# The copies of the rope outputs to the heads are issued by ACT, behind the weight splits, instead of by the sync engine

## The chip, the cores and the metric

The kernel runs on one core of a Trainium2 chip. A core has five engines with instruction streams of their own: TensorE (PE, matmuls), VectorE (DVE), ScalarE (ACT), GpSimd (POOL) and the sync engine (SP), and 16 DMA engines that move what the engines' streams tell them to. The metric is the time of one execution on the device, in microseconds; lower is better.

## The reference

Two blocks follow each other on 256 tokens of width 1024. The first has two layers, and it is in these that the change lies. Cut to what matters:

```python
def hybrid_layer(x, norm_g, w_in, ...):
    h = rmsnorm(x, norm_g)
    proj = h @ w_in        # q and k of three kinds of attention, v, gates
    ...
    # every q and k: apply_rope(heads(t, n), cos, sin)
    #   x1, x2 = halves of a head of 64; [x1*c - x2*s, x1*s + x2*c]
    ya = moba_attention(...); yb = dsa_attention(q, k, v, iq, ik, iw); yc = dilated_mixture(...)
    return x + merged @ w_out
```

dsa_attention needs index scores of iq and ik for all tokens before it can choose its 64 keys each. The second block (feed-forward, Fourier and retention layers, with conditioning rows from ada_w) is untouched.

## The kernel before

All matmuls are in fp32 precision made of two halves: a weight tile is split in a high part (w_high, by ACT) and a low part (w_low, by POOL), and TensorE does three products per pair. The weights stream through a ring of four slots (RING). A chunk of the stream goes SP load to raw (chunk, L476), ACT split to w_high (split, L603), POOL subtraction to w_low (L1107), 24 matmuls L1984 to L1986 (12 matmuls L2033 to L2035 for a v chunk). The load of chunk m waits for lo_done of chunk m - 4, the split waits for landed of its slot and for chunk_done of chunk m - 4. ACT and POOL work three chunks ahead (AHEAD).

A layer is a chain of such phases: qk (24 chunks, six laps of four), vn (12 v chunks), mix (32 chunks interleaved with the softmax units), br, out. In qk, DVE turns each pair of result banks into rope outputs (rotate, L1279 to L1284) in the tile rot, and multiplies rows of ada_w between them (modulate, L1289 and L1293). rot holds head halves by chunk; the attention needs whole heads of 64 rows on one side of the partitions. So small SBUF to SBUF copies move rot to heads: for each group g of four chunks eight copies of 32 partitions (heads_of, L496, 64 KB each), six groups per layer, and four copies of 32 KB for the last index key tile (L536). All 52 add to the semaphore heads_in. Before, SP issues them in one piece per group between the weight loads: groups 0 to 2 in the qk laps 3 to 5, groups 3 to 5 and the four last copies in the three vn laps. The loads of the first mix chunks stand behind these in SP's order.

In vn DVE also makes the normed input again: normed_scaled (L1416) for tile k, then ACT's high part (L769, two tiles behind the splits of v chunks 7 to 10), then DVE's low part (L1422). At the end of vn TensorE waits for all copies of the layer, `e.wait_ge(heads_in, 832 * L + 832)` (L2075), and computes the index scores (L2090). ACT applies relu (L773, L776), which stands in its order behind the splits of mix chunks 0, 1 and 2, and the first mix chunk on TensorE waits for the first relu (`relu_done`), since it uses the bank.

Of the kernel before, what the change touches and what calls it, by code (L numbers as in the profile page):

```python
# [30 lines left out]
RING = 4  # L31
AHEAD = 3
# [7 lines left out]
W8 = ((CW, LINE),) * RING  # L40
WIDE = ((CW, 0),) * RING
WV = ((2 * VW, 0),) * RING
# [9 lines left out]
QK, VN, GATE, MIXG, BR, OUT = 24, 12, 8, 24, 8, 8  # L52
# [104 lines left out]
@contextmanager  # L157
def turns(eng, count, *tallies):

    kept = [(t, t.base, t.n) for t, _ in tallies]  # L160
    with eng.Fori(0, count) as i:
        for t, k in tallies:
            t.base = t.base + i * k
        yield i
    for (t, base, n), (_, k) in zip(kept, tallies):
        assert t.n - n == k, (t.n - n, k)
        t.base, t.n = base, n + k * count


def program(nc, xT_d, cols_d, cond_d, ada_d, w1_d, wv_d, wu_d, wd_d, w2_d, rope_d, mask_d, ident_d, identb_d,  # L170
            dft_d, rope2_d, dist_d, out_d):
    with ExitStack() as ctx:
# [274 lines left out]
        def of_layer(name, L):  # L447
            m, d, a, n = hybrid[name]
            return m + L * PER_LAYER, d + L * PER_D, a, n
# [18 lines left out]
        def _(e):  # L468
# [18 lines left out]
                e.dma_start(ada[:, slot, :], ada_d[bass.ds(r, 1)].rearrange("a p n -> p (a n)"))\  # L487
                    .then_inc(ada_landed[slot], 16)

            def heads_of(d0, g):  # L490

                e.wait_ge(emptied_d, 4 + d0 + RING * g + RING)
                for jq in range(4):
                    for r in range(2):
                        dst = 64 * (jq % 2) + 32 * r
                        e.dma_start(head_tiles[dst:dst + 32, bass.ds(2 * g, 2), jq // 2, :],  # L496
                                    rot_tiles[32 * jq:32 * jq + 32, bass.ds(2 * g, 2), r, :]).then_inc(heads_in, 16)

            head_tiles = heads[:, 0:NPOS // 2, :].rearrange("p (g a) t -> p g a t", a=2)
            rot_tiles = rot[:, :, :].rearrange("p (g a) t -> p g a t", a=2)  # L500
            per = PER_LAYER - VN
            for L in range(LAYERS):
                m0, d0, _, _ = of_layer("qk", L)
                w0, r0 = per * L, ADA_L * L
                for j in range(RING):
                    chunk(m0 + j, j, W8, w1_d, w0 + j)
                    if L == 0 and j == 0:
                        for k in range(4):
                            e.dma_start(x[:, 0, 2 * k:2 * k + 2, :], xT[:, 2 * k:2 * k + 2, 0:T]).then_inc(x_in[k], 16)
                if L:  # L510
                    e.wait_ge(ada_done, 2 + r0)
                e.dma_start(ada[:, :, :], cond_d).then_inc(cond_in, 16)
                if L == 0:
                    for dst, src in ((rope[:, :, :], rope_d.rearrange("p (a t) -> p a t", a=2)),
                                     (ident[:, :], ident_d), (identb[:, :], identb_d), (mask[:, :], mask_d)):
                        e.dma_start(dst, src).then_inc(consts_in, 16)
                for i in range(1, QK // RING):
                    for j in range(RING):
                        chunk(m0 + RING * i + j, j, W8, w1_d, w0 + RING * i + j)
                        if j % 2:  # L520
                            if i == 1 and j == 1:
                                e.wait_ge(c_silu, 2 * L + 2)
                            ada_row(r0 + 2 * (i - 1) + j // 2, j // 2)
                    if i >= 3:
                        heads_of(d0, i - 3)
                m1 = m0 + QK
                for i in range(VN // RING):
                    for j in range(RING):
                        chunk(m1 + RING * i + j, j, WV, wv_d, VN * L + RING * i + j)
                        if i == 0 and j % 2:  # L530
                            ada_row(r0 + ADA_L - 2 + j // 2, j // 2)
                    heads_of(d0, QK // RING - 3 + i)
                for jq, half in ((2, 1), (3, 0)):
                    for r in range(2):
                        dst = 64 * half + 32 * r
                        e.dma_start(heads[dst:dst + 32, NPOS // 2, :],  # L536
                                    rot[32 * jq:32 * jq + 32, QK - 2 + r, :]).then_inc(heads_in, 16)
                load(m1 + VN, 2 * RING, W8, w1_d, w0 + QK)
                if L == LAYERS - 1:
                    e.wait_ge(ada_done, 2 + ADA_H)  # L540
                    e.dma_start(x[:, 1, :, :], xT[:, :, T:2 * T]).then_inc(context_in, 16)
                load(m1 + VN + 2 * RING, MIX + BR + OUT - 2 * RING, W8, w1_d, w0 + QK + 2 * RING)
# [51 lines left out]
        def _(e):  # L594
            n_sq, n_scaled, n_shifted = Tally(), Tally(), Tally()

            def split(lap, mm, c, width):

                e.wait_ge(landed[c % RING], 16 * lap + 16)
                if not (isinstance(mm, int) and mm < RING):  # L600
                    e.wait_ge(chunk_done, 1 + mm - RING + 1)
                w, at_ = width
                e.activation(wh[:, c % RING, at_:at_ + w], raw[:, c % RING, 0:w], ACT.Copy).then_inc(hi_done, 1)  # L603
# [24 lines left out]
            def stepped(base, widths, after, first, count, before=None, behind=None):  # L628

                m0, _, _, n = base  # L630
                for k in range(first, first + count):
                    i, j = divmod(k, RING)
                    c = j + AHEAD
                    w = after if k + AHEAD >= n else widths
                    if before:
                        before(k)
                    split(hybrid_lap(m0) + i + c // RING, m0 + RING * i + c, c, w[c % RING])
                    if behind:
                        behind(k)
# [7 lines left out]
            def to_hh(k, q):  # L647
                return flat(hh, k, T * q, T)


            def table_for_sqrt():
                e.activation(spare[:, 4:5], eps[:, :], ACT.Sqrt)
# [79 lines left out]
            for L in range(LAYERS):  # L732
                def laps(name):
                    lap_of[0] = hybrid[name][0] // RING + L * (PER_LAYER // RING)
                    return of_layer(name, L)
# [17 lines left out]
                stepped(laps("qk"), W8, WV, 0, RING, roots, silu_of_cond)  # L753
                i_end = QK // RING - 1
                m0 = laps("qk")[0]
                with turns(e, i_end - 1) as i:
                    for j in range(RING):
                        c = j + AHEAD
                        split(lap_of[0] + i + 1 + c // RING, m0 + RING + RING * i + c, c, W8[0])
                stepped(laps("qk"), W8, WV, RING * i_end, RING)  # L760


                m0 = laps("vn")[0]
                for c in range(AHEAD, VN + AHEAD):
                    split(lap_of[0] + c // RING, m0 + c, c, WV[0] if c < VN else W8[0])
                    if 0 <= c - TILES_FROM < KT // 2:
                        for k in (2 * (c - TILES_FROM), 2 * (c - TILES_FROM) + 1):
                            e.wait_ge(scaled, n_scaled())
                            e.activation(hh[:, k, 0:T], ps[:, 6 + k % 2, 0:T], ACT.Copy).then_inc(norm_hi, 1)  # L769
# [1944 lines left out]
```

## Time and profile before

| | us |
|---|---|
| median of 3 runs | 2269.53 (2267.81 to 2269.68) |
| the profiled execution | 2268.79 |
| its span in the trace | 2267.0 |
| PE busy | 2211.4 |
| DVE, ACT, POOL busy | 1124.1, 830.8, 1342.6 |

The page's header gives the span. Busy time is the union of an engine's instruction times; matmuls are pipelined, so a busy PE need not be at its peak. Register, semaphore and DMA-issuing instructions don't count as busy. Layer 0 has its qk and vn phases from 14 to 112 us, layer 1 from 305 to 402 us.

### The profile page before, as it was taken

Reading aid. Unit: us, or ns where it says so; the run is one execution under the profiler, and the core shown is the slowest. Engines: PE = TensorE matmul, PEld = TensorE weight load, DVE = VectorE, ACT = ScalarE, POOL = GpSimd, SP = SyncE. Lnnn points to the kernel's source line nnn. Section 1 sums busy time; section 2 is a strip of 40 time slices with the busy share of each in tenths; the row PEclk is TensorE's granted clock in tenths of the full one; section 3 lists DMA queues with packets and bytes.
Section 4 is the critical chain, followed back from the end, with each engine's and each line's share of the span. In section 5 each row is a group of like instructions: output and inputs, shape, how many; then the busy total and the mean of one; then the engine's idle time right before and its main releaser. Section 6 shows DMA issues by size and latency. Waiting matters only on the chain.

```text
span 2267.0 us, 39013 instructions
## 1 busy us (share of the span) xinstructions
PE 2211.4 (98%) x13460; PEld 1971.0 (87%) x13460; DVE 1124.1 (50%) x2117; ACT 830.8 (37%) x1270; POOL 1342.6 (59%) x704
## 2 busy tenths in 40 slices
PE   8989999899999999999999999999999999999999
PEld 7989999898888888878888888888888988999999
DVE  6754568544665543277655423655522511243653
ACT  5355453554532222243222222322222413665444
POOL 6765787648665554323655544555544644558997
PEclk9999999999999999999999999999999999999999
DMA  8842468523365543312655432555533422225555
GB/s 289 276 152 96 147 242 278 189 90 131 117 238 200 196 147 95 103 66 86 223 186 199 137 103 92 203 192 185 195 90 95 163 103 102 103 84 186 182 169 159
DMA packets 112399, 356.35 MB, mean 157 GB/s; under 512 B 13224, under 2 KB 21928, under 8 KB 111920
## 3 DMA queue, kind: packets, MB, share of 16 engines
q1 hardware_dynamic: 112304, 355.07, 46.5%
q8 instruction: 61, 1.00, 0.2%
q14 instruction: 34, 0.28, 0.0%
HBM read 347.40 MB, written 1.05 MB: 154 GB/s over the span
## 4 chain that ended last, share of the span: by engine, by line
PE 82%; DVE 6%; issue 4%; POOL 3%; ACT 2%; DMA 1%; SPq 1%; DVEq 0%; POOLq 0%; ACTq 0%
PE ps L1984 22%; PE ps L1985 22%; PE ps L1986 22%; POOL w_low L1107 3%; PE ps L2033 1%; PE ps L2035 1%; PE ps L2034 1%; PE ps L2152 1%; PE ps L2485 1%; PE ps L2120 1%; DMA raw<-in_w_dram 1%; DVE ps L1347 1%; PE ps L2185 1%; PE ps L1996 1%; SPq L496 1%
## 5 line engine op out<-in xcount | busy, mean ns | idle before, releaser
L1107 POOL TENSOR_TENSOR w_low<-raw,w_high 128x1024 fp32r<-128x1024 f32 (+3 forms) x542 | 1200.3, 2224 | 663.7 <-ACT w_high L603 662.6
L603 ACT ACTIVATE w_high<-raw 128x1024 fp32r<-128x1024 f32 (+3 forms) x544 | 537.3, 989 | 1060.6 <-PE ps L1986 823.3
L1984 PE MATMUL ps<-h_high,w_high 128*128 128x256 f32 (+2 forms) x2704 | 889.2, 329 | 16.9 <-DVE rot L1284 5.1
L1985 PE MATMUL ps<-h_low,w_high 128*128 128x256 f32 (+2 forms) x2704 | 879.4, 325 | 0.0
L1986 PE MATMUL ps<-h_high,w_low 128*128 128x256 f32 (+2 forms) x2704 | 879.2, 325 | 0.0
L1984 PEld LDWEIGHTS ps<-h_high,w_high 128*128 128x128 f32 x2704 | 511.8, 189 | 65.3 <-DVE rot L1284 6.1
L1985 PEld LDWEIGHTS ps<-h_low,w_high 128*128 128x128 f32 x2704 | 512.8, 190 | 42.9
L1986 PEld LDWEIGHTS ps<-h_high,w_low 128*128 128x128 f32 x2704 | 513.0, 190 | 42.6
L1984 PE MATMUL ps<-act_high,w_high 128*128 128x512 f32 (+1 forms) x770 | 266.2, 346 | 0.0
L1985 PE MATMUL ps<-act_low,w_high 128*128 128x512 f32 (+1 forms) x770 | 265.6, 345 | 0.0
L1986 PE MATMUL ps<-act_high,w_low 128*128 128x512 f32 (+1 forms) x770 | 265.6, 345 | 0.0
L1188 POOL TENSOR_TENSOR act_low<-hn,act_high 128x512 f32 (+3 forms) x88 | 101.8, 1157 | 213.2 <-DVE act_high L1636 205.6
L1633 DVE TENSOR_TENSOR hn<-tn,ps 128x512 f32<-128x512 f32 x66 | 45.4, 689 | 287.0 <-PE ps L1986 258.1
L1984 PEld LDWEIGHTS ps<-act_high,w_high 128*128 128x128 f32 x770 | 145.1, 188 | 18.3
L1985 PEld LDWEIGHTS ps<-act_low,w_high 128*128 128x128 f32 x770 | 145.1, 188 | 18.1
L1986 PEld LDWEIGHTS ps<-act_high,w_low 128*128 128x128 f32 x770 | 145.1, 188 | 18.0
L1306 DVE SCALAR_TENSOR_TENSOR sq<-ada,ps 128x1024 f32<-128x1024 f32 x120 | 146.5, 1221 | 17.2
L1302 DVE SCALAR_TENSOR_TENSOR sq<-ada,ps 128x1024 f32<-128x1024 f32 x120 | 146.1, 1218 | 9.6 <-DMA ada<-in_ada_dram 1.3
L1661 DVE SCALAR_TENSOR_TENSOR x<-ps,gate,x 128x256 f32 (+1 forms) x49 | 21.8, 481 | 257.1 <-PE ps L1986 256.7
L1996 PE MATMUL ps<-h_high,w_high 128*128 128x256 f32 (+1 forms) x264 | 79.3, 300 | 15.1 <-DVE h_low L1245 7.8
L2033 PE MATMUL ps<-w_high,h_high 128*128 128x512 f32 (+1 forms) x224 | 83.7, 373 | 2.0 <-POOL w_low L1107 2.0
L2035 PE MATMUL ps<-w_high,h_low 128*128 128x512 f32 (+1 forms) x224 | 83.3, 372 | 0.0
(243 smaller groups left out, 2272.8 us busy)
## 6 DMA issues: line engine op xcount, KB each, us to landing
raw<-in_w_dram SPq DMA_DIRECT2D x216, 512.0 KB, 3.4
raw<-in_wu_dram SPq DMA_DIRECT2D x176, 512.0 KB, 4.2
ada<-in_ada_dram SPq DMA_DIRECT2D x144, 512.0 KB, 3.6
raw<-in_wd_dram SPq DMA_DIRECT2D x64, 384.0 KB, 3.1
raw<-in_wd_dram SPq DMA_DIRECT2D x64, 320.0 KB, 2.9
raw<-in_wv_dram SPq DMA_DIRECT2D x24, 408.0 KB, 5.0
heads<-rot SPq DMA_DIRECT2D x96, 64.0 KB, 3.4
ada<-in_cond_dram SPq DMA_DIRECT2D x6, 512.0 KB, 4.8
```

What stands on the lines that cost most here:

```text
L603: e.activation(wh[:, c % RING, at_:at_ + w], raw[:, c % RING, 0:w], ACT.Copy).then_inc(hi_done, 1)
L1107: e.tensor_tensor(wl[:, c % RING, at_:at_ + w], raw[:, c % RING, 0:w], wh[:, c % RING, at_:at_ + w].bitcast(F32), ALU.subtract).then_inc(l ...
L1188: e.tensor_tensor(flat(al, 2 * i + j // 2, 0, halves * T), hn[:, j // 2, 0:halves * T], flat(ah, 2 * i + j // 2, 0, halves * T).bitcast(F3 ...
L1302: e.scalar_tensor_tensor(out=trash, in0=ada2[half][:, :], scalar=1.0, in1=cond_bank(0), op0=ALU.mult, op1=ALU.mult, accum_out=mod[:, bass. ...
L1306: e.scalar_tensor_tensor(out=trash, in0=ada2[half][:, :], scalar=1.0, in1=cond_bank(1), op0=ALU.mult, op1=ALU.mult, accum_out=mod[:, bass. ...
L1633: e.tensor_tensor(hn[:, j, 0:w], tn[:, j, 0:w], ps[:, 2 * j + 1, 0:w], ALU.mult)\
L1984: e.matmul(ps[:, bank, to:to + n], wh[:, j, w], hi, start=(first and t == tiles[0]), stop=False)
L1985: e.matmul(ps[:, bank, to:to + n], wh[:, j, w], low, start=False, stop=False)
L1986: end = e.matmul(ps[:, bank, to:to + n], wl[:, j, w], hi, start=False, stop=(last and t == tiles[-1]))
L1996: e.matmul(out, wh[:, j, w], hi, start=first, stop=False)
L2033: e.matmul(out, hh[:, k, tok], wh[:, j, w], start=(first and t == 0), stop=False)
L2035: end = e.matmul(out, hl[:, k, tok], wh[:, j, w], start=False, stop=(last and t == 1))
```

## The change

The copies leave SP's stream and enter ACT's. heads_of now takes the quarter jq and issues two copies; it is called behind each split, so that eight copies of a group are spread over four splits: group 0 behind the splits of chunks 15 to 18, and so on; group 5 behind the splits of v chunk 11 and of mix chunks 0, 1 and 2. The four single copies follow behind the last of these. The wait on DVE's rotation stands before the first pair of a group. The loop over qk laps is written out for this in all but its first two laps.

```diff
-            def heads_of(d0, g):
-
-                e.wait_ge(emptied_d, 4 + d0 + RING * g + RING)
-                for jq in range(4):
-                    for r in range(2):
-                        dst = 64 * (jq % 2) + 32 * r
-                        e.dma_start(head_tiles[dst:dst + 32, bass.ds(2 * g, 2), jq // 2, :],
-                                    rot_tiles[32 * jq:32 * jq + 32, bass.ds(2 * g, 2), r, :]).then_inc(heads_in, 16)
-
...
-                    if i >= 3:
-                        heads_of(d0, i - 3)
...
-                    heads_of(d0, QK // RING - 3 + i)
-                for jq, half in ((2, 1), (3, 0)):
-                    for r in range(2):
-                        dst = 64 * half + 32 * r
-                        e.dma_start(heads[dst:dst + 32, NPOS // 2, :],
-                                    rot[32 * jq:32 * jq + 32, QK - 2 + r, :]).then_inc(heads_in, 16)
...
+            def heads_of(d0, g, jq):
+                if jq == 0:
+                    e.wait_ge(emptied_d, 4 + d0 + RING * g + RING)
+                for r in range(2):
+                    dst = 64 * (jq % 2) + 32 * r
+                    e.dma_start(head_tiles[dst:dst + 32, 2 * g:2 * g + 2, jq // 2, :],
+                                rot_tiles[32 * jq:32 * jq + 32, 2 * g:2 * g + 2, r, :]).then_inc(heads_in, 16)
+
...
-                with turns(e, i_end - 1) as i:
+                d0 = of_layer("qk", L)[1]
+                with turns(e, 2) as i:
                     for j in range(RING):
                         c = j + AHEAD
                         split(lap_of[0] + i + 1 + c // RING, m0 + RING + RING * i + c, c, W8[0])
-                stepped(laps("qk"), W8, WV, RING * i_end, RING)
+                for i in range(2, i_end - 1):
+                    for j in range(RING):
+                        c = j + AHEAD
+                        split(lap_of[0] + i + 1 + c // RING, m0 + RING + RING * i + c, c, W8[0])
+                        heads_of(d0, i - 2, j)
+                stepped(laps("qk"), W8, WV, RING * i_end, RING, None, lambda k: heads_of(d0, i_end - 3, k % RING))
 
 
                 m0 = laps("vn")[0]
                 for c in range(AHEAD, VN + AHEAD):
                     split(lap_of[0] + c // RING, m0 + c, c, WV[0] if c < VN else W8[0])
+                    if c - AHEAD < 3 * RING:
+                        heads_of(d0, i_end - 2 + (c - AHEAD) // RING, (c - AHEAD) % RING)
+                    if c == VN + AHEAD - 1:
+                        for jq, half in ((2, 1), (3, 0)):
+                            for r in range(2):
+                                dst = 64 * half + 32 * r
+                                e.dma_start(heads[dst:dst + 32, NPOS // 2, :],
+                                            rot[32 * jq:32 * jq + 32, QK - 2 + r, :]).then_inc(heads_in, 16)
```

## Rows read from the trace of the kernel before

**Rows 1.** The page: chain that ended last; DMA issues (median us to landing last).
```profile
PE ps L1984 22%; PE ps L1985 22%; PE ps L1986 22%; POOL w_low L1107 3%; PE ps L2033 1%; PE ps L2035 1%; PE ps L2034 1%; PE ps L2152 1%; PE ps L2485 1%; PE ps L2120 1%; DMA raw<-in_w_dram 1%; DVE ps L1347 1%; PE ps L2185 1%; PE ps L1996 1%; SPq L496 1%
...
raw<-in_w_dram SPq DMA_DIRECT2D x216, 512.0 KB, 3.4
```
**Rows 2.** Busy time by stretch: PE, PEld, DVE, ACT, POOL, then PEclk, DMA share, GB/s.
```profile
34.00:103.00 69.00, 68.71 (x521) 68.28 (x521) 56.37 (x96) 26.91 (x32) 56.65 (x26) 1.00 0.89 288
...
330.00:399.00 69.00, 68.53 (x505) 68.14 (x503) 56.16 (x94) 26.58 (x34) 56.34 (x26) 1.00 0.87 286
```
**Rows 3.** Timeline of PE: start us, us, instruction, idle before it and its releaser.
```profile
103.87 0.45 PE L2033 MATMUL ps<-w_high,h_high 128*128 128x408 f32 x1 [0.44 <-POOL w_low L1107]
...
109.45 0.45 PE L2033 MATMUL ps<-w_high,h_high 128*128 128x408 f32 x1 [0.85 <-POOL w_low L1107]
...
111.88 1.58 PE L2090 MATMUL ps<-heads 64*128 64x128 f32 x16
115.38 0.38 PE L1984 MATMUL ps<-h_high,w_high 128*128 128x256 f32 x1 [1.92 <-ACT relu L773]
...
399.29 0.45 PE L2033 MATMUL ps<-w_high,h_high 128*128 128x408 f32 x1 [0.76 <-POOL w_low L1107]
...
401.72 1.58 PE L2090 MATMUL ps<-heads 64*128 64x128 f32 x16
403.55 0.39 PE L1984 MATMUL ps<-h_high,w_high 128*128 128x256 f32 x1 [0.25 <-ACT relu L773]
```
**Rows 4.** Timeline of ACT at the end of vn, both layers.
```profile
106.51 0.88 ACT L603 ACTIVATE w_high<-raw 128x816 fp32r<-128x816 f32 x1
...
113.78 1.06 ACT L603 ACTIVATE w_high<-raw 128x1024 fp32r<-128x1024 f32 x1 [0.18 <-DMA raw<-in_w_dram]
114.74 0.58 ACT L773 ACTIVATE relu<-ps 128x512 f32<-128x512 f32 x1
...
396.35 0.88 ACT L603 ACTIVATE w_high<-raw 128x816 fp32r<-128x816 f32 x1
```
**Rows 5.** The tile raw, 106 to 116 us: SP's loads, ns min/median/max.
```profile
L476 SPq DMA_DIRECT2D raw<-in_w_dram x5: 332/349/760, 106.3 to 113.8; - x5
```
**Rows 6.** Timeline of SP at the end of vn, layer 0.
```profile
98.34 5.07 SPq L496 DMA_DIRECT2D heads<-rot  x8
103.45 2.49 SPq L536 DMA_DIRECT2D heads<-rot  x4
106.33 3.57 SPq L476 DMA_DIRECT2D raw<-in_w_dram  x4
```
**Rows 7.** Timeline of POOL at the end of vn, both layers.
```profile
101.59 4.32 POOL L1107 TENSOR_TENSOR w_low<-raw,w_high 128x816 fp32r<-128x816 f32 x2 [1.56 <-ACT w_high L603]
...
391.49 4.25 POOL L1107 TENSOR_TENSOR w_low<-raw,w_high 128x816 fp32r<-128x816 f32 x2 [1.64 <-ACT w_high L603]
```
**Rows 8.** Copies by line: ns min/median/max, first and last start; landing of L536's.
```profile
L496 SPq DMA_DIRECT2D heads<-rot x96: 586/597/1741, 45.8 to 392.0; - x96
...
DMA to landing us min/median/max: 1.8/1.8/1.9
```
**Rows 9.** ACT at 716 us: a split, and the register instruction behind it.
```profile
716.44 1.07 ACT L603 ACTIVATE w_high<-raw 128x1024 fp32r<-128x1024 f32 x1 [3.90 <-PE ps L1986]
...
L599 ACTq FUSED_REGOPS  x1: 46/46/46, 716.4 to 716.4; - x1
```
**Rows 10.** PE after an idle time; and stretches: PE busy, PEclk, DMA share, GB/s.
```profile
453.35 0.29 PE L2152 MATMUL ps<-vn,probT 128*128 128x64 f32 x1 [2.98 <-DVE y L1512]
...
116.90:120.30 3.40, 3.40 (x19) 0.50 0.65 202
...
454.80:458.20 3.40, 3.40 (x18) 0.50 0.00 0
```
**Rows 11.** Timeline of DVE in the norm chain, layer 0.
```profile
100.69 0.49 DVE L1416 SCALAR_TENSOR_TENSOR ps<-x,cols,rs 128x256 f32<-128x256 f32 x1
...
104.47 1.73 DVE L1416 SCALAR_TENSOR_TENSOR ps<-x,cols,rs 128x256 f32<-128x256 f32 x1
```

More of the change, by code:

```diff
@@ L488, in ada_row @@
                     .then_inc(ada_landed[slot], 16)
-            def heads_of(d0, g):
-                e.wait_ge(emptied_d, 4 + d0 + RING * g + RING)
-                for jq in range(4):
-                    for r in range(2):
-                        dst = 64 * (jq % 2) + 32 * r
-                        e.dma_start(head_tiles[dst:dst + 32, bass.ds(2 * g, 2), jq // 2, :],
-                                    rot_tiles[32 * jq:32 * jq + 32, bass.ds(2 * g, 2), r, :]).then_inc(heads_in, 16)
-            head_tiles = heads[:, 0:NPOS // 2, :].rearrange("p (g a) t -> p g a t", a=2)
-            rot_tiles = rot[:, :, :].rearrange("p (g a) t -> p g a t", a=2)
             per = PER_LAYER - VN
@@ L648, in to_hh @@
                 return flat(hh, k, T * q, T)
+            head_tiles = heads[:, 0:NPOS // 2, :].rearrange("p (g a) t -> p g a t", a=2)
+            rot_tiles = rot[:, :, :].rearrange("p (g a) t -> p g a t", a=2)
+            def heads_of(d0, g, jq):
[5 more added lines that the diff above has]
+                                rot_tiles[32 * jq:32 * jq + 32, 2 * g:2 * g + 2, r, :]).then_inc(heads_in, 16)
             def table_for_sqrt():
```

## Prediction, made before the changed kernel was run

> **What bounds the kernel now.** The page comes first [rows 1]: TensorE is busy for 2211.4 of 2267.0 us (98%), and the first three shares of the chain that ended last, 22% each, are its chunk matmuls, so a microsecond counts only where TensorE stands idle. The sync engine's head copies (L496) hold 1% of that chain, and the two places to look at are the two projection stages. The table by stretches [rows 2] says where in them TensorE has a gap: 68.71 of 69.00 us busy from 34 to 103 us in layer 0, and 68.53 of 69.00 from 330 to 399 us in layer 1. In these stretches SP issues eight copies per lap ahead of weight loads, and some splits wait for those loads, yet the loads reach TensorE in time. What SP would give back there is hidden. The open ground is behind it.
>
> TensorE's own timeline [rows 3] splits that up. Layer 0: 0.44 and 0.85 us before v chunks 9 and 11, both for POOL's low part, then the index scores L2090 at 111.88, then 1.92 us for the relu L773, so the first mix chunk starts at 115.38. Layer 1: 0.76 us, L2090 at 401.72, 0.25 us for the relu, first mix chunk at 403.55. Why was the relu late? In ACT's order [rows 4] it stands behind the splits of the first three mix chunks, the last at 113.78, each of which waited for its load. The loads were late because SP had first to issue twelve copies, 98.34 to 105.94, and started them at 106.33 [rows 6]. In layer 1 it is the same, but TensorE waits 0.25 us only. So the most that the change could return is small: 0.44 + 0.85 + 1.92 in layer 0 and 0.76 + 0.25 in layer 1, 4.2 us, and a clock fall (below).
>
> **What the change removes.** 52 issues per layer leave SP, each 0.64 us of its time (8 in 5.07 us and the next at 103.45 [rows 6]). In the loaded stretches that is worth nothing to TensorE, by [rows 2]. At the end SP is free, and the load of mix chunk 2 goes out when POOL has done the low part of v chunk 10 (its slot): 101.59 + 4.32 = 105.91 in layer 0, 391.49 + 4.25 = 395.74 in layer 1 [rows 7]. With 0.15 us for SP and the 3.4 us median landing of such a load [rows 1], it is there at 109.5 and 399.3, where ACT took it at 113.78 in layer 0. Taken alone this half is a gain.
>
> **What it adds.** The same 52 issues go to ACT, two behind each split. No trace here has an issue from ACT; the nearest row is the same copy issued from SP, 0.60 us each with a pitch of 0.64 [rows 6, 8]. I take that. Its ends: 0.33 us, SP's bare weight load [rows 5], and 1.74, the longest copy issue [rows 8]. Is ACT's computing in the way? A register instruction behind a split that had waited 3.90 us for TensorE stands at 716.4, the very start of that split at 716.44, not at its wait's begin [rows 9]. So a waiting split holds back all that stands behind it, and once it has started (not ended) the next may run. Issues then run beside the split's own 0.88 to 1.06 us [rows 4], and splits can follow each other at 2 x 0.64 = 1.3 us instead of 1.0. A v chunk takes TensorE 2.4 us (109.45 to 111.88 [rows 3]), a qk chunk with its 24 matmuls more, so ACT keeps up and I cost the first 40 issues of a layer at nothing on TensorE; cover is the wait that ACT has between splits. If it failed, it would be a gap before each chunk. The one place with little cover is the norm chain: the norm tiles L769 wait for DVE, and one behind a split can be held for what is left of its two issues. Those tiles mostly wait for DVE anyway, so I take 0 and bound it by 0 to 1 us in all. The waits on the rotation ahead of each group are for laps that DVE left long ago.
>
> **The tail is where the price is.** The scores L2090 wait for all 52 copies. Before, the last was issued at 105.35 and landed 1.8 us later [rows 6, 8], well ahead of 111.88. Now ACT issues the last two of group 5 and the four single tiles (L536) behind the split of mix chunk 2, which itself waits for a load. Counted from the split of v chunk 11, which waits for DVE's norm chain (106.51 and 396.35 [rows 4]):
> - Layer 0: mix 0 at 107.8, mix 1 at 109.1, mix 2 at 110.4 (its load is there at 109.5, v chunk 10 of its slot is done 0.85 before 109.45, at 108.60 [rows 3]). Six issues: the last begins 5 x 0.64 later, 113.6, and lands 1.8 later at 115.4. From L2090 to the first mix chunk it was 403.55 - 401.72 = 1.83 with the relu close behind, so mix begins at 117.3, against 115.38: +1.9.
> - Layer 1: 397.65, 398.95, 400.25 (load 399.3, chunk 10 done 399.29 - 0.76 = 398.53), last issue 403.45, landed 405.25, mix at 407.1 against 403.55: +3.5.
> TensorE has no slack behind this (98% busy), so both shift the end one to one.
>
> **The clock.** The granted clock stood at its lower level (0.50 of 2.4 GHz, 1.2) for 3.4 us after TensorE had idled 2.98 us before 453.35, and in layer 0 after the 1.92 us before 115.38 [rows 3, 10]. Each such stretch does 1.7 us less work. After another idle time as long as the first it did not fall, so a fall is likely, not sure. Layer 0 keeps its fall. In layer 1 TensorE would now stand for about 405.25 - 401.72 = 3.5 us, and I count one new fall: +1.7.
>
> **What comes back.** With loads no longer in bunches behind the copies, POOL's low parts spread out and cross DVE's norm chain less: one tile of L1416 takes 1.73 us in most rows and 0.49 at 100.69, in the 1.56 us that POOL idled before 101.59 [rows 7, 11]. That moves the split of v chunk 11 forward. An estimate, from the 1.24 us between these two: one slow tile fewer in layer 0 and half of one in layer 1, 1.9 us at most, and 0 at least since POOL has as much to do as before. I take half, -0.9. The gaps before v 9 and 11 may close, but the copies decide then and not these.
>
> **Sum.** 1.9 + 3.5 + 1.7 - 0.9 = +6.2 us on the profiled execution's 2268.79: 2275.0. That execution is 0.74 under the median of the three runs, 2269.53, so I forecast 2275.7 for the median, +0.27%. The likeliest case's own range: full return and no fall 1.9 + 3.5 - 1.9 = +3.5; no return, norm tiles late, a second fall 7.1 + 1.0 + 1.7 = +9.8; so 2272.5 to 2279.5.
>
> **Rivals.**
> 1. Faster: the norm chain escapes POOL. It is the return above, but larger. Each L1416 that runs clear saves 1.73 - 0.49 = 1.24 us and brings v 11, the issues and L2090 forward. At 2.7 us a layer without a new fall the copies' delay is paid off; at four tiles, 5.0 us, L2090 is bound by TensorE again: layer 0 gives 0.44 + 0.85 + (3.50 - 1.83) = 3.0 and its fall of 1.7, layer 1 gives 0.76, 5.4 in all, 2264. For it: some tiles already run clear. Against: POOL is busy 56.65 of 69.00 us in this stretch [rows 2], so they must meet somewhere.
> 2. No measurable change: ACT's issues are not held by a waiting split. Then the last six follow the end of v chunk 10 (108.60 and 398.53): last issue 111.8 and 401.7, landed 113.6 and 403.5, mix at 115.4 and 405.35: 0 and +1.8, with or without a fall, 2269.5 to 2273. [rows 9] speak against it, but for a register instruction, not for a copy.
> 3. Much slower: an issue from ACT waits until the running split has ended. Then each split costs 1.06 + 1.28 = 2.34 (v: 2.16). Layer 0: 108.7, 111.0, 113.4, first of six at 114.4, last 117.6, landed 119.4, mix 121.3, +5.9; layer 1 likewise 411.1, +7.5; the norm chain is held too, an estimated 1.4 in each (one split and its issues, 2.16, less what a tile waits anyway), and 1.7 for the fall: +18, 2287. Against: the next instruction starts 0.1 us ahead of a split's end even now (ACT 113.78 + 1.06, L773 at 114.74 [rows 4]), and the register instruction at its start.
>
> The Trainium skill speaks for rival 2: Perfetto Trace Analysis, section Per-instruction lifecycle, says that an ACT instruction is pushed to a wait queue and the sequencer is then ready for the next one while the semaphores are still open. By that rule the sum would be 0 to +3.5 us instead of +6.2. The trace's [rows 9] disagree with it here, so it gets the smaller chance. The same skill, DMA: Bandwidth & Descriptors, section Issuing engines are not separate DMA queues, says that issuing from several engines saves only sequencer time, usually small beside the transfer. Here 0.60 us stands beside 3.4 us of landing, but twelve in a row were 7.6 us; the trace agrees only in that TensorE did not see most of it.
>
> **Chances.** Forecast 0.50, rival 1 0.18, rival 2 0.19, rival 3 0.13. About 0.2%, 4.5 us, is what a measurement of this kernel can tell from no change: slower begins at 2274.07. Of the forecast's 0.50 four fifths lie above it: slower 0.40 + 0.13 = 0.53; same 0.10 + 0.19 = 0.29; faster 0.18. The range goes from 2265 to 2284: it leaves out two thirds of rival 1 and two thirds of rival 3, 0.2 together.
>
> **What would show it.** In the changed trace: ACT's copies at 0.6 us each, two after each split start (price, rivals 2 and 3: look whether they begin at the split's start, before it, or at its end); TensorE idle before L2090 and not before the first mix chunk, about 3.5 us in each layer (the tail); L2090 at 115.4 and 405.3; a lower clock behind it in layer 1; SP's first mix loads by 101 to 106 and 390 to 396; L1416's slow rows five or six of eight (the return); no new gap from 34 to 100 us (the cover). The forecast is wrong if L2090 starts within a microsecond of the last v chunk, or if a gap opens in the qk laps.

## The result, and the profile after

| | before | after |
|---|---|---|
| median, 5 runs each, side by side | 2269.53 | 2283.03 |
| its runs | 2265.93 to 2273.07 | 2280.37 to 2283.95 |
| the profiled execution | 2268.79 | 2283.95 |
| its span | 2267.0 | 2282.2 |
| mean granted clock over the span | 0.996 | 0.991 |

The changed kernel is slower by 0.6%: ratio 1.006, interval 1.0048 to 1.0072, +13.5 us. The direction and the place were forecast, the size was +6.2: the median lies above the 2272.5 to 2279.5 us that the likeliest case was given, and inside the whole range of 2265 to 2284 by 1 us. One execution of the kernel before, beside the first four experiments, took 2447.93 us at a granted clock of 0.85 and is left out of every median below. Lines have moved: the split is L584, POOL's low part L1113, the copies L639 (groups) and L770 (the four singles), the relus L779 and L782, the chunk matmuls L1990 to L1992, the v chunks L2039, the scores L2096.

The page of the changed kernel: the chain that ended last, and the DMA issues with their median landing, against [rows 1]. The last line is the same row of DMA issues on the page of the kernel before.

```profile
PE ps L1990 24%; PE ps L1991 24%; PE ps L1992 24%; POOL w_low L1113 2%; PE ps L2039 1%; PE ps L2040 1%; PE ps L2041 1%; PE ps L2158 1%; PE ps L2491 1%; PE ps L2126 1%; PE ps L2002 1%; DVE ps L1353 1%; PE ps L2191 1%; PE ps L2529 1%; PE ps L2531 1%
...
heads<-rot ACTq DMA_DIRECT2D x96, 64.0 KB, 4.2
...
heads<-rot SPq DMA_DIRECT2D x96, 64.0 KB, 3.4
```

SPq, 1% of the chain before, is gone from it, as the change wants, and the time is longer all the same. The chain names no new culprit: the new wait is only some 14 us of 2282. What is to be seen is the copies' row. The 96 group copies land 4.2 us after their issue in the median. I had taken 1.8 for the last ones, from the single copies [rows 8], but the group copies landed 3.4 us after theirs before the change already (2.0 to 5.6). That row was there to be read and stands neither in my rows nor in the sum.

The table by stretches of the changed kernel, columns as in [rows 2]: first the two loaded stretches, then three at the lower clock.

```profile
34.00:103.00 69.00, 69.00 (x521) 68.96 (x520) 54.95 (x96) 26.32 (x32) 56.46 (x26) 0.98 0.89 284
341.00:410.00 69.00, 68.81 (x508) 68.42 (x506) 56.09 (x94) 28.13 (x34) 56.35 (x26) 1.00 0.92 285
114.70:124.90 10.20, 4.38 (x23) 3.56 (x24) 0.00 (x0) 2.00 (x3) 1.97 (x1) 0.50 0.56 160
169.30:176.10 6.80, 5.97 (x27) 5.13 (x28) 3.83 (x15) 2.30 (x6) 2.37 (x1) 0.50 0.26 85
415.10:421.90 6.80, 3.24 (x18) 2.42 (x18) 0.05 (x1) 0.86 (x2) 2.32 (x2) 0.50 0.67 224
```

The stretch with the first 39 copies of layer 0, and that with the first 44 of layer 1, cost TensorE nothing: 69.00 and 68.81 of 69.00 us busy, against 68.71 and 68.53 in [rows 2]. Behind them, at the end of vn, stands what is new. TensorE's timeline there:

```profile
109.76 0.45 PE L2039 MATMUL ps<-w_high,h_high 128*128 128x408 f32 x1 [0.69 <-POOL w_low L1113]
...
120.52 2.93 PE L2096 MATMUL ps<-heads 64*128 64x128 f32 x16 [8.28 <-DMA heads<-rot]
123.38 0.58 PE L1990 MATMUL ps<-h_high,w_high 128*128 128x256 f32 x1
...
410.51 0.45 PE L2039 MATMUL ps<-w_high,h_high 128*128 128x408 f32 x1 [0.71 <-POOL w_low L1113]
...
418.66 2.93 PE L2096 MATMUL ps<-heads 64*128 64x128 f32 x16 [5.64 <-DMA heads<-rot]
421.52 0.56 PE L1990 MATMUL ps<-h_high,w_high 128*128 128x256 f32 x1
```

TensorE idles 8.28 and 5.64 us for the copies (forecast 3.5 in each layer), and the scores then take 2.93 us at the lower clock where they took 1.58 [rows 3]. Set beside [rows 3], this gives the account by subtraction of the starts of the same matmul, v chunk 11 and the first mix matmul of each layer:

| stretch | after minus before | share |
|---|---|---|
| start to v chunk 11, layer 0 | 109.76 - 109.45 | +0.3 |
| to mix 0, layer 0 | 123.38 - 115.38 = 8.00 | +7.7 |
| to v chunk 11, layer 1 | 410.51 - 399.29 = 11.22 | +3.2 |
| to mix 0, layer 1 | 421.52 - 403.55 = 17.97 | +6.8 |
| to the end | 15.2 | -2.8 |

The two tails are 14.5 of 15.2 us; the rest, +0.3, +3.2 and -2.8, nearly cancels. (The +0.3 is itself a difference of two things, told below under what comes back.) ACT's timeline shows how the tails come about: first one pair from the qk laps, then the end of vn in layer 0, then the three splits for mix in layer 1.

```profile
78.88 0.89 ACT L584 ACTIVATE w_high<-raw 128x816 fp32r<-128x816 f32 x1 [1.94 <-PE ps L1992]
78.89 1.24 ACTq L639 DMA_DIRECT2D heads<-rot  x2
...
106.53 0.39 ACT L775 ACTIVATE h_high<-ps 128x256 fp32r<-128x256 f32 x1 [1.71 <-DVE ps L1422]
106.62 0.59 ACTq L639 DMA_DIRECT2D heads<-rot  x1
...
107.97 1.06 ACT L584 ACTIVATE w_high<-raw 128x1024 fp32r<-128x1024 f32 x1 [0.28 <-issue]
107.98 2.51 ACTq L639 DMA_DIRECT2D heads<-rot  x2
110.59 1.06 ACT L584 ACTIVATE w_high<-raw 128x1024 fp32r<-128x1024 f32 x1 [1.57 <-issue]
110.61 1.24 ACTq L639 DMA_DIRECT2D heads<-rot  x2
112.14 1.06 ACT L584 ACTIVATE w_high<-raw 128x1024 fp32r<-128x1024 f32 x1 [0.49 <-DMA raw<-in_w_dram]
112.15 1.24 ACTq L639 DMA_DIRECT2D heads<-rot  x2
113.42 2.54 ACTq L770 DMA_DIRECT2D heads<-rot  x4
...
408.73 1.06 ACT L584 ACTIVATE w_high<-raw 128x1024 fp32r<-128x1024 f32 x1 [0.29 <-issue]
...
410.14 1.06 ACT L584 ACTIVATE w_high<-raw 128x1024 fp32r<-128x1024 f32 x1 [0.35 <-PE ps L2041]
...
411.61 1.06 ACT L584 ACTIVATE w_high<-raw 128x1024 fp32r<-128x1024 f32 x1 [0.41 <-DMA raw<-in_w_dram]
```

The split at 78.88 had waited 1.94 us for TensorE, and its two copies begin at 78.89: with the split, neither before it (rival 2) nor at its end (rival 3, the split at 112.14 runs to 113.20 and its copies begin at 112.15). Where no wait holds the split, a copy can begin a little sooner: the split of v chunk 11 stood at 106.81 behind a norm tile that ran until 106.92, and its first copy began at 106.62. So it is the split's wait that holds the copies. The order was read rightly, then. What came after the last issue was not. The four single copies of each layer, and SP beside them in layer 0 (two views):

```profile
L770 ACTq DMA_DIRECT2D heads<-rot x8: 612/612/617, 113.4 to 414.8; - x8
...
DMA to landing us min/median/max: 3.2/4.2/5.1
```
```profile
106.41 10.80 SPq L476 DMA_DIRECT2D raw<-in_w_dram  x5
```

The last issues are at 113.42 + 3 x 0.64 = 115.3 and at 414.8; the scores start at 120.52 and 418.66, that is 5.2 and 3.8 us later. Before, SP's bunch of twelve copies kept the loads away: the first load of mix went out at 106.33, 0.4 us behind the end of the last copy's issue [rows 6], and that copy landed at 107.2. Now five loads of 512 KB leave SP from 106.41 to 117.2, while ACT's last copies go out.

### The profile page after: what moved, and what is told of

Same layout as the page of the kernel before. It is cut to its first block, busy times and chain, and to the rows that moved or that the text cites. A ratio compares the mean times of both kernels' runs of the same rounds, so it can differ in the third digit from the quotient of the medians.

```text
span 2282.2 us, 38997 instructions
## 1 busy us (share of the span) xinstructions
PE 2217.1 (97%) x13460; PEld 1975.7 (87%) x13460; DVE 1119.7 (49%) x2117; ACT 832.0 (36%) x1270; POOL 1344.3 (59%) x704
## 4 chain that ended last, share of the span: by engine, by line
PE 87%; DVE 5%; issue 2%; POOL 2%; ACT 2%; DMA 1%; DVEq 0%; ACTq 0%; SPq 0%; POOLq 0%
PE ps L1990 24%; PE ps L1991 24%; PE ps L1992 24%; POOL w_low L1113 2%; PE ps L2039 1%; PE ps L2040 1%; PE ps L2041 1%; PE ps L2158 1%; PE ps L2491 1%; PE ps L2126 1%; PE ps L2002 1%; DVE ps L1353 1%; PE ps L2191 1%; PE ps L2529 1%; PE ps L2531 1%
## 5 line engine op out<-in xcount | busy, mean ns | idle before, releaser
L1113 POOL TENSOR_TENSOR w_low<-raw,w_high 128x1024 fp32r<-128x1024 f32 (+3 forms) x542 | 1201.7, 2224 | 678.2 <-ACT w_high L584 677.1
L584 ACT ACTIVATE w_high<-raw 128x1024 fp32r<-128x1024 f32 (+3 forms) x544 | 537.4, 989 | 1060.1 <-PE ps L1992 866.2
L1990 PE MATMUL ps<-h_high,w_high 128*128 128x256 f32 (+2 forms) x2704 | 890.3, 329 | 15.7 <-DVE rot L1290 5.9
L1992 PE MATMUL ps<-h_high,w_low 128*128 128x256 f32 (+2 forms) x2704 | 880.0, 325 | 0.0
L1990 PEld LDWEIGHTS ps<-h_high,w_high 128*128 128x128 f32 x2704 | 513.9, 190 | 64.6 <-DVE rot L1290 6.7
L1992 PEld LDWEIGHTS ps<-h_high,w_low 128*128 128x128 f32 x2704 | 512.4, 190 | 42.6
L1990 PE MATMUL ps<-act_high,w_high 128*128 128x512 f32 (+1 forms) x770 | 266.2, 346 | 0.0
L1992 PE MATMUL ps<-act_high,w_low 128*128 128x512 f32 (+1 forms) x770 | 265.6, 345 | 0.0
L1990 PEld LDWEIGHTS ps<-act_high,w_high 128*128 128x128 f32 x770 | 145.0, 188 | 18.4
L1992 PEld LDWEIGHTS ps<-act_high,w_low 128*128 128x128 f32 x770 | 145.0, 188 | 18.0
L2039 PE MATMUL ps<-w_high,h_high 128*128 128x512 f32 (+1 forms) x224 | 83.4, 372 | 1.4 <-POOL w_low L1113 1.4
```

The source lines that it names most:

```text
L1113: e.tensor_tensor(wl[:, c % RING, at_:at_ + w], raw[:, c % RING, 0:w], wh[:, c % RING, at_:at_ + w].bitcast(F32), ALU.subtract).then_inc(l ...
L1990: e.matmul(ps[:, bank, to:to + n], wh[:, j, w], hi, start=(first and t == tiles[0]), stop=False)
L1992: end = e.matmul(ps[:, bank, to:to + n], wl[:, j, w], hi, start=False, stop=(last and t == tiles[-1]))
L2039: e.matmul(out, hh[:, k, tok], wh[:, j, w], start=(first and t == 0), stop=False)
```

## The experiments

Every kernel ran beside the kernel before on the same chip: the first four together (before: 2270.99), the next three together (before: 2270.97), the last by itself (before: 2273.71).

### Which of the copies cost

Groups 0 to 4 stay on ACT, group 5 and the four singles go back to SP, at the end of vn and ahead of the mix loads.

```diff
+                heads_of(d0, QK // RING - 1)      # on SP, and the four singles
                 load(m1 + VN, 2 * RING, W8, w1_d, w0 + QK)
...
-                    if c - AHEAD < 3 * RING:
+                    if c - AHEAD < 2 * RING:
                         heads_of(d0, i_end - 2 + (c - AHEAD) // RING, (c - AHEAD) % RING)
-                    if c == VN + AHEAD - 1:
```

> Of the changed kernel, only the last twelve issues of each layer (group 5 and the four single tiles) go back to SP, where they stood before; the 40 issues of groups 0 to 4 stay on ACT. Theory A (the whole price is the tail: the last issues stand behind the split of mix chunk 2 and land late, and the scores wait for them): the scores start right behind the last v chunk in both layers, near 112 and 402 us, the first mix chunk near 115 and 404, and the time is that of the kernel before, 2267 to 2272 us. Theory B (each issue costs ACT, and through it TensorE, something in every lap): 40 of 52 issues still cost, some 10 of the 13.5 us, about 2280.

Measured: 2271.89, ratio 1.0004 (0.9992 to 1.0015). Its TensorE, layer 0, and the landing of the singles:

```profile
110.77 1.58 PE L2107 MATMUL ps<-heads 64*128 64x128 f32 x16
113.42 0.38 PE L2001 MATMUL ps<-h_high,w_high 128*128 128x256 f32 x1 [1.06 <-ACT relu L790]
```
```profile
L534 SPq DMA_DIRECT2D heads<-rot x8: 584/592/672, 101.5 to 397.9; - x8
...
DMA to landing us min/median/max: 1.8/1.9/2.0
```

The reverse: SP issues groups 0 to 4 as before, ACT issues group 5 and the singles only.

```diff
+                    if i >= 3:
+                        heads_of(d0, i - 3)       # on SP, as before, for groups 0 to 4
...
-                    if c - AHEAD < 3 * RING:
+                    if 2 * RING <= c - AHEAD < 3 * RING:
```

> The complement: groups 0 to 4 are issued by SP as before, and ACT issues only group 5 and the four single tiles, where the changed kernel does. Theory A: the scores wait for the copies as in the changed kernel, 5 to 9 us before L2090 in each layer, 2279 to 2284 us. Theory B: 12 of 52 issues, some 3 us, 2272 to 2273.

Measured: 2286.54, ratio 1.0078 (1.0063 to 1.0093). The waits are in the first reading's band, the time is 2.5 us above it. TensorE:

```profile
119.42 2.93 PE L2110 MATMUL ps<-heads 64*128 64x128 f32 x16 [7.33 <-DMA heads<-rot]
...
416.89 2.93 PE L2110 MATMUL ps<-heads 64*128 64x128 f32 x16 [7.76 <-DMA heads<-rot]
```

Together they settle it. Forty of the 52 copies of a layer are free on ACT (+0.9 us, the interval holds 0), and the last twelve alone carry the whole price (+15.6 us against +13.5 for all 52; the intervals overlap). The first 40 don't pay either: with them gone from SP the time stays where it was. Note the 1.06 us in front of mix 0 in the first of these two kernels: with twelve issues ahead of its loads SP is late again and so is the relu, as in [rows 3].

### The landing: copies beside weight loads

The changed kernel, but SP holds the load of mix chunk 3, and all after it, until the layer's copies have landed.

```diff
-                load(m1 + VN, 2 * RING, W8, w1_d, w0 + QK)
+                for j in range(3):
+                    chunk(m1 + VN + j, j, W8, w1_d, w0 + QK + j)
+                e.wait_ge(heads_in, 832 * L + 832)
+                chunk(m1 + VN + 3, 3, W8, w1_d, w0 + QK + 3)
+                load(m1 + VN + RING, RING, W8, w1_d, w0 + QK + RING)
```

> The changed kernel, but SP waits for all copies of the layer (heads_in) before it loads mix chunk 3, so no weight load is in flight beside the last copies. Theory A with its second part (the last copies land 5.1 and 3.8 us after their issue instead of 1.8 because SP's weight loads, no longer held, share the DMA engines with them): they land 1.8 to 2.6 us after issue, the scores start 2 to 3 us sooner in each layer, and the time falls by 3 to 6 us to 2277 to 2280. Rival (a copy issued by ACT lands late of itself, whatever else is in flight): the landing stays at 4 to 5 us and the time at 2283.

Measured: 2281.16, ratio 1.005 (1.0036 to 1.0064), 1.2 us above the first reading's band. The singles, TensorE at the scores, and ACT:

```profile
L774 ACTq DMA_DIRECT2D heads<-rot x8: 612/612/617, 110.7 to 408.4; - x8
...
DMA to landing us min/median/max: 1.8/1.9/1.9
```
```profile
114.58 2.93 PE L2100 MATMUL ps<-heads 64*128 64x128 f32 x16 [5.39 <-DMA heads<-rot]
...
410.33 2.93 PE L2100 MATMUL ps<-heads 64*128 64x128 f32 x16 [5.26 <-DMA heads<-rot]
```
```profile
109.43 1.06 ACT L588 ACTIVATE w_high<-raw 128x1024 fp32r<-128x1024 f32 x1 [2.92 <-DMA raw<-in_w_dram]
109.44 1.24 ACTq L643 DMA_DIRECT2D heads<-rot  x2
```

The same eight copies, from the same engine, land in 1.8 to 1.9 us instead of 3.2 to 5.1. That they land late in the changed kernel is therefore the loads' doing and not that of ACT's queue. TensorE's wait in layer 0 falls from 8.28 to 5.39 us. In layer 1 it falls by 0.4 only, since mix 2 itself came late: its load was 4.9 us on the way (issued at 400.31), in layer 0 5.0 (issued at 104.43), and the split that waits for it (109.43 in layer 0) holds the last six copies. The price beside the kernel before falls from 13.5 to 10.2 us, as much as the 2.9 + 0.4 of the two waits, but the two intervals overlap, and the stretches at the lower clock lie differently (one at 460.8 that the changed kernel doesn't have). So the landing is shown as a cause, and its worth in the end time is not measured to better than a few us.

The changed kernel, each of the four single copies in two halves: as many bytes, four issues more.

```diff
+                                for lo in (0, T // 2):
+                                    e.dma_start(heads[dst:dst + 32, NPOS // 2, lo:lo + T // 2],
+                                                rot[32 * jq:32 * jq + 32, QK - 2 + r, lo:lo + T // 2])\
+                                        .then_inc(heads_in, 16)
```

> The changed kernel, each of the four single copies of a layer split into two of half the columns: the same bytes in four more issues per layer, all behind the split of mix 2. Theory A (the scores wait for the end of a row of issues at 0.6 us each): last issue 2.4 us later (117.7 instead of 115.3 in layer 0), scores 2.4 us later a layer, so +4.8 us over the changed kernel: 2286 to 2290 us, if the scores' clock is the same. Rival B (the landing beside the weight loads sets the end, not the number of issues; the added issues overlap the slow landing of the earlier ones): scores less than 1 us later a layer, 2282 to 2285 us.

Measured: 2287.13, ratio 1.0073 (1.0056 to 1.0089). ACT in layer 0, then TensorE:

```profile
109.76 5.11 ACTq L771 DMA_DIRECT2D heads<-rot  x8
```
```profile
118.57 2.93 PE L2098 MATMUL ps<-heads 64*128 64x128 f32 x16 [9.43 <-DMA heads<-rot]
...
418.44 2.93 PE L2098 MATMUL ps<-heads 64*128 64x128 f32 x16 [9.20 <-DMA heads<-rot]
```

A half costs ACT the same 0.64 us as a whole: 5.11 us for eight against 2.54 for four. TensorE's wait grows by 1.15 us in layer 0 and 3.55 in layer 1, 4.7 in all, as the row of issues wants (2.6 twice would be 5.1), though the two layers don't share it as expected. The time lies in the band of the first reading, but its price beside the kernel before, 16.2 us against 13.5, is 2.7 us more and the intervals overlap, so the time alone would not decide.

### Where the last copies may stand

All 52 on ACT, but four issues behind each split from vn on, so that the last stands behind a split of vn.

```diff
+                    n = c - AHEAD
+                    if n < 6:
+                        for jq in (2 * (n % 2), 2 * (n % 2) + 1):
+                            heads_of(d0, i_end - 2 + n // 2, jq)
+                    if n == 6:       # the four singles
```

> All 52 issues stay on ACT, but in the vn laps four stand behind each split instead of two, so that group 5 is out behind the splits of v chunks 7 and 8 and the single tiles behind that of v chunk 9 (near 101 us in layer 0). Theory A: all copies have landed by 106 us and its like in layer 1, the scores start right behind the last v chunk, and SP's mix loads are not held either, so the relu comes at once: first mix chunk near 113.5 to 114.5 in layer 0, one clock fall fewer, 2262 to 2269 us, below the kernel before. Theory B: as many issues on ACT and denser (4 x 0.64 = 2.6 us against 2.4 for a v chunk), so 2280 us or more, with gaps between the v chunks.

Measured: 2269.48, ratio 0.9995 (0.9981 to 1.0009), 0.5 us above the first reading's band. Its mix 0 starts at 116.81 in layer 0, not at 113.5 to 114.5. ACT, then TensorE, layer 0:

```profile
100.23 1.91 ACTq L639 DMA_DIRECT2D heads<-rot  x3
102.19 0.38 ACT L777 ACTIVATE h_high<-ps 128x256 fp32r<-128x256 f32 x1 [1.28 <-issue]
```
```profile
103.07 0.42 PE L2041 MATMUL ps<-w_high,h_high 128*128 128x408 f32 x1 [0.72 <-POOL w_low L1115]
106.74 0.45 PE L2041 MATMUL ps<-w_high,h_high 128*128 128x408 f32 x1 [1.22 <-POOL w_low L1115]
112.88 0.45 PE L2041 MATMUL ps<-w_high,h_high 128*128 128x408 f32 x1 [0.99 <-POOL w_low L1115]
115.30 1.58 PE L2098 MATMUL ps<-heads 64*128 64x128 f32 x16
```

The scores no longer wait, and all 13.5 us are gone. There is no gain over the kernel before, though: four issues to a split (three of them in the row shown) hold the next part of the norm chain by 1.28 us, and TensorE pays 2.93 us in three gaps, where it had been 1.29 in two [rows 3]. The issues are free only while they fit beside the split and what the chain leaves.

With three behind each split the row ends earlier too: three of the four single copies stand behind the split of v chunk 11 and the last one behind that of mix 0 (not behind v chunk 11, as the expectation says), so none stands behind the splits of mix 1 and mix 2.

```diff
+                    for n in range(3 * (c - AHEAD), 3 * (c - AHEAD) + 3):
+                        if n < 24:
+                            one_head(d0, i_end - 2 + n // 8, n % 8 // 2, n % 2)
+                        elif n < 28:
+                            single(n - 24)
```

> All 52 copies on ACT as in the changed kernel, but from the first split in vn three issues behind each split instead of two, so that the last of them stands behind the split of v chunk 11 and not behind mix 2. Groups 0 to 2 as in the changed kernel. Theory A (a copy costs nothing on ACT as long as the issues behind a split fit into the split's slack, and what cost in the changed kernel is the end of the row): last issue at 106 to 109 us, landed by 111 to 112.5, scores at 111.9 to 112.5 with no or a short wait, and no gaps ahead of the v chunks over 0.5 us, where four a split made gaps of 0.7 to 1.3: 2268 to 2271 us. Rival B (any issue more than two a split already delays the next split on the path): gaps of 0.5 us or more ahead of several v chunks and 2272 to 2276 us.

Measured: 2263.54, ratio 0.9979 (0.9963 to 0.9995), 4.5 us below the band of either reading. And the same program again:

> The same program as three a split, once more, on another day's chip, because its interval against the kernel before ended only 0.0005 below 1 and its single times reached from 2259 to 2275 us. Theory A (the gain over the kernel before is the earlier end of vn, about 3.4 us in layer 0 as its profile showed, with the scores at about 110.4 us and no wait before them): ratio 0.997 to 0.999. Rival B (what its profiled run gained was two fewer stretches at the lower clock, which shift with any shift of the program and are luck): ratio within 0.001 of 1.

Measured: 2268.35 beside 2273.71, ratio 0.9975 (0.9961 to 0.9989). TensorE in the first of the two, then in the second:

```profile
110.44 1.58 PE L2103 MATMUL ps<-heads 64*128 64x128 f32 x16
```
```profile
110.33 0.45 PE L2046 MATMUL ps<-w_high,h_high 128*128 128x408 f32 x1 [0.85 <-POOL w_low L1120]
113.32 1.58 PE L2103 MATMUL ps<-heads 64*128 64x128 f32 x16 [0.48 <-DMA heads<-rot]
```

This is the one placement of those tried that beats the kernel before, by 0.2% (twice, and both intervals end below 1). The first profile fits the reading that the scores come early: they start at 110.44 against 111.88 and the relu is ready, so that mix 0 starts at 111.95 instead of 115.38. The second profile fits it worse, with a gap and a short wait in layer 0, mix 0 at 114.8, and mix 0 of layer 1 at 404.94 against 403.55 before; yet its ratio is the same. So the gain is shown, and the early end of vn as its source is not. Luck with the lower clock explains little of it: over all executions the mean granted clock is 0.9953 against 0.9954 beside it in the first of the two, and 0.9953 against 0.9947 in the second, an estimated 1.4 of 5.4 us.

Last, the kernel before with nothing on ACT, its copies spread on SP: two behind each chunk load, three in the last lap of vn.

```diff
+                        if i >= 3:
+                            heads_of(d0, i - 3, j)        # two copies behind each load
...
+                        heads_of(d0, QK // RING - 3 + i, j)
+                        if i == 2:
+                            single(j)
```

> The kernel before, its copies still issued by SP and none by ACT, but spread: two behind each chunk load instead of eight behind every fourth, and in the last lap of vn three behind each load, the last of each three being one of the four single copies. Theory A (the whole price of the change is that the last twelve issues stand behind splits that wait, and lie beside the weight loads when they land; an early end of the copies is worth what it takes off the start of the loads for mix): SP never holds a load back by eight issues of 0.6 us, so the last copy is issued at about 101 to 103 us in layer 0, the loads for mix start at about 104 instead of 106.3, the scores start at 111 to 112 as before, and mix 0 begins at 113.5 to 115.4: 2264 to 2271 us. Rival B (copies on a queue that also carries loads land late wherever they stand): the spread copies delay the v chunks' loads each by two issues of 0.6 us and the scores come at 114 or later: 2273 to 2280 us.

Measured: 2268.38, ratio 0.9995 (0.9985 to 1.0005), in the band of the first reading. TensorE, layer 0:

```profile
102.62 0.45 PE L2036 MATMUL ps<-w_high,h_high 128*128 128x408 f32 x1 [0.73 <-POOL w_low L1110]
108.21 0.45 PE L2036 MATMUL ps<-w_high,h_high 128*128 128x408 f32 x1 [0.87 <-POOL w_low L1110]
110.64 1.58 PE L2093 MATMUL ps<-heads 64*128 64x128 f32 x16
```

The relu's 1.92 us [rows 3] is gone here too, mix 0 starts at 112.15, and still the median is not to be told from that of the kernel before. What SP's bunches cost is as small as the prediction put it.

The same kernel shows whose doing a late landing is from the other side. All its copies come from SP, with SP's own loads between them; the single ones:

```profile
L502 SPq DMA_DIRECT2D heads<-rot x8: 593/594/602, 92.0 to 390.4; - x8
...
DMA to landing us min/median/max: 2.4/4.2/4.7
```

That is as late as from ACT in the changed kernel (3.2/4.2/5.1), and the group copies here take 6.0 us in the median. It costs nothing here only because the last one is issued at 99.71 and has landed at 103.6, 7 us ahead of the scores.

## Why the prediction was right in direction and short in size

**What bounds it.** Right. No microsecond of the loaded stretches was to be had, and 14.5 of the 15.2 us came at the end of vn.

**The removal.** Right that SP's issues were hidden. Moving forty of them to ACT gave 1.0004.

**The issue's price and its hold.** Right, and the choice among rivals with it: 0.59 to 0.62 us each from ACT (0.60 taken from SP's rows), and the order by [rows 9], which the pair at 78.88 and 78.89 confirms. Perfetto Trace Analysis of the Trainium skill, section Per-instruction lifecycle, would have had the sequencer go on while the split waits; for DMA issues behind a waiting split the trace disagrees. The pair at 78.88 doesn't decide that, since the wait for TensorE is there an instruction of its own (L582, at 78.82) ahead of the split; the run with the loads held does, where that instruction was done at 106.99, the split waited for its load until 109.43, and its copies began at 109.44. One size was off: one copy in layer 0 took up to 1.86 us, as the pair at 107.98 (2.51 us) shows, and put the split of mix 1 at 110.59. The 1.74 of [rows 8] was there as the upper end, and I took the median for all.

**The tail.** The step that failed. In layer 1, less the 11.22 us by which v chunk 11 is late, its terms can be read one by one:

| layer 1 | forecast | measured less 11.22 |
|---|---|---|
| split of mix 0 | 397.65 | 397.51 |
| split of mix 1 | 398.95 | 398.92 |
| split of mix 2 | 400.25 | 400.39 |
| last issue | 403.45 | 403.6 |
| landed, scores start | 405.25 | 407.44 |
| mix 0 | 407.1 | 410.30 |

Up to the last issue nothing is off by more than 0.2 us. The term that was mis-sized is the landing: 1.8 us [rows 8] came from rows of the kernel before in which hardly a load was in flight, and the change is just what lets loads run beside the last copies. It was 3.8 us here and 5.2 in layer 0, and 1.9 again when the loads were held. The group copies of the kernel before, 3.4 us in the median with loads in flight, were the nearer row; with 3.4 in place of 1.8 in both layers the sum would have been an estimated +9.4. The second is the 1.83 us from the scores to mix 0: it was 2.86 in both layers, as the wait put the scores themselves at the lower clock. In layer 0 the slow copy adds its 1.3 us to the row and the landing 3.4: last issue 115.3 (forecast 113.6), landed 120.5 (115.4), mix 0 at 123.4 (117.3).

**The clock.** I counted one stretch more at the lower clock, 1.7 us. In the tails there were 10.2 and 6.8 us of it, of which much lay in idle time and cost nothing; TensorE did work in it that took 1.35 us longer in each layer for the scores alone. Elsewhere the stretches moved. The kernel before had them at 116.9, 424.1, 454.8, 557.2 and 605.0; the changed one, outside the tails, at 32.8, 169.3, 568.7, 616.5 and 1019.3. The one at 169.3 is part of the +3.2 us between the tails, the missing ones of 424.1 and 454.8 part of the -2.8 behind them. The kernel with only the tail on ACT has them at 167.5, 566.8, 614.6 and 1017.4, each some 1.9 us earlier, and lacks the one at 32.8. That looks as if they followed from how far the tail shifts the program, but two things speak against it. The stretch at 32.8 stands ahead of the first copy (50.6), so the copies have no part in it. And the one program with three a split had stretches at 33.6, 320.3 and 446.6 in its first profile and at 159.6, 449.8, 555.6 and 603.4 in its second. No run here gives a rule by which to tell them ahead: this part of the cause stays open.

**What comes back.** It came in layer 0, and did not reach the end. Four of the eight norm tiles of layer 0 ran at 0.48 to 0.49 us, where it had been two, and DVE's chain of them, from the start of the first to that of the last, took 10.2 us (94.54 to 104.77) instead of 11.2 (93.27 to 104.47). But it began 1.3 us later: TensorE is late by that much from 38 us on, behind the stretch at the lower clock at 32.8. So ACT's last norm tile is at 106.53, and it was at 106.23; these two make the +0.3 of the table. In layer 1 four of eight ran clear as before, and nothing came back. Rival 1 falls with it: it needed 2.7 us a layer.

**The rivals.** Rivals 2 and 3 fall by where the copies begin. Rival 3's 2287 is nearest in number to what was measured, by another mechanism: the number alone would have misled. It is also only for its sake that the whole range reached up to 2284: that the measured time lies in it is luck and no merit of the sum.

**The sum once more**, by the profiled execution: +0.3, +7.7, +3.2, +6.8 and -2.8 make +15.2. Forecast for the tails were 1.9 and 3.5. Of the 9.1 us that they came out higher, the landing makes 3.4 + 2.0, the scores' lower clock 2 x 1.03 and the slow issue with what followed it 1.4 (115.34 - 113.6, less the 0.3 of the start): 8.9 together.

## What to carry to other kernels

A DMA issue moved behind an instruction that waits is as late as that instruction, so before moving a row of them, find the last one and the wait ahead of it; the early ones cost nothing and buy nothing. When a bunch of small transfers moves out from among the big loads, it no longer keeps the loads away while it lands: price the landing from rows with loads in flight. Such rows can be in the trace already, under another line of the same copies. The cure was to leave the engine and to put three instead of two behind each split, so that the row ends two splits earlier, with none behind those of mix 1 and mix 2; four already held up the engine's own work.

## What the runs showed of the hardware that was not expected

- Copies of 32 KB inside the chip's SBUF land in 1.8 to 2.0 us by themselves and in 3.2 to 5.1 us with 512 KB loads in flight. It is the loads that count and not whose queue the copies are in: issued by SP between its own loads they took 2.4 to 4.7 us. It goes both ways: the loads of mix 2 in the run with the loads held, in flight with copies and nearly alone of the loads, took 5.0 and 4.9 us where the median is 3.4. DMA: Bandwidth & Descriptors of the Trainium skill, section Issuing engines are not separate DMA queues, says that issuing from several engines saves only sequencer time. The trace agrees that nothing more is gained, and shows that something can be lost: the copies that stood in a bunch ahead of the loads now land beside them.
- An issue has its price by the instruction and not by the bytes: 0.64 us of pitch for a copy and for half of one.
- One issue of a copy now and then takes 1.1 to 1.9 us instead of 0.6, on SP before [rows 8] as on ACT. In three of the four kernels with the tail on ACT it was one of the copies behind v chunk 11 or mix 0 of layer 0. What holds it isn't shown by any run here.
